# A two-layer encoder step on Trainium2: where the turned k and v tiles are emptied relative to the exponentials, and which bank the first v turn uses

## The chip, the cores and the metric

The kernel runs on one core of one Trainium2 chip. The metric is the device time of one execution in microseconds (us). Before the change it was 2435.56 us, the median of 3 runs (2432.95 to 2436.89).

A core has TensorE (PE in the profile; its weight loads are PEld), VectorE (DVE), ScalarE (ACT), GpSimd (POOL), and SyncE (SP), which only issues DMAs here. Each takes its own instructions in the order in which they are written. The engines keep each other in order by semaphores only.

## The reference

Two token groups (512 prompt tokens and 32 sample tokens with a cache of 256) pass through two layers. Each layer is SwiGLU, a mixer, SwiGLU, each with norms and gains. The first layer's mixer is "ab": eight heads of band attention with a relative-position bias (a) and four heads of differential attention (b). The second layer's is "c": sixteen heads of causal attention with a forget bias. The keys and values are results too, with tokens in rows.

```
proj = h @ w_in                      # q, k, v of every head
s = q @ k.T * 64 ** -0.5 + bias      # a: relative position, b: ALiBi, c: forget
p = softmax(s)                       # b: p0 - lam * p1
out = (p @ v) @ w_out
new = (k, v)                         # also returned
```

## The kernel before

Everything is held with features on the partitions and 544 tokens in the free dimension. A weight tile is split into a high and a low part (`split` and `half_split`: ACT writes `w_hi`, DVE the rest `w_lo`), and every product is three matmuls, written for two halves of 272 tokens.

Each mixer runs in nine **stages** (`Stage`, `st` 0 to 8). Stage `st` projects k, v and q of the head pair `st` (`lin_chunk`, three units of eight tiles), and at the same time attends with the head pair `st - 1`. In mixer ab the attending kind alternates: stages 1, 3, 5, 7 are a, stages 2, 4, 6, 8 are b. In mixer c all of 1 to 8 are c. Stage 0 only projects (`head`), stage 8 only attends. So 14 stages both project and attend: 4 of kind a, 3 of kind b, 7 of kind c.

A stage is a loop over steps `s` = 0 to 15 on each engine, and the order within a step is written out by hand. Steps 0 to 3 project k, 4 to 7 v, 8 to 11 q, two tiles a step. On PE a step is: the two tiles, `transpose_probs` of attention tile `s - lag` (lag 2, in b 3, where only odd tiles are turned), the products with v (`values` or `pair_values`), and in even steps below 10 `scores(s)` and `scores(s + 1)`. On ACT `exps(s)`, which is the exponential of tile `s`, and after it `split_next` (in steps 4, 5, 8, 9 half a weight tile) end the step.

Besides that each stage has three **turns** (`turn` on PE, `empty_turn` on ACT). k (`kT`), then v (`vT`), is transposed by four matmuls with the identity, and ACT copies it into `k_nat` or `v_nat`; the third turn does the sample's 32 rows and the cache's keys (`ckT`). Before, PE does them at the head of steps 5, 9 and 12, and ACT empties them at the head of the same steps, so behind the exponential and the weight half of the step before. All turns and all transposed probabilities go through one PSUM bank, `ps_t`. `tr_plan` numbers them, `wait_tr` makes PE wait until ACT has emptied the one before (semaphore `tr_out`), and `tr_ps` tells ACT that one is written. `ps_o`, another bank, takes the products with v.

The lines of the profile of before: L1278 the projection's matmuls, L1300 the turns of k and v, L1303 and L1306 the third turn, L1328 the scores, L1349 the transposes of probabilities, L1377 and L1400 the products with v, L1478 a turn of the forget terms, L1528 the weight half on ACT, L1829 the copies into `k_nat` and `v_nat`, L1841 the copy of transposed probabilities, L1853 the exponential, L1960 a whole `w_lo`, L2434 the row maximum for which the exponential waits.

Of the kernel before, what the change touches and what calls it, by code (L numbers as in the profile page):

```python
# [17 lines left out]
P = 128  # L18
# [7 lines left out]
QT = SEQ // P  # L26
# [191 lines left out]
def program(nc, ins, outs):  # L218
# [43 lines left out]
    with ExitStack() as ctx:  # L262
# [395 lines left out]
        def by_vector(n):  # L658
# [331 lines left out]
        def _(pe):  # L990
# [270 lines left out]
            def stage(st):  # L1261
# [22 lines left out]

                def turn(step):

                    new, base = st.new, st.at("tr")
                    if st.st == 0 and step == 5:
                        pe.wait_ge(pre_done, 2 * KT * (st.j + 1))
                    if step == 5:  # L1290
                        pe.wait_ge(kv_evac, evs + 1)
                        src = kT[:, new, :]
                    elif step == 9:
                        pe.wait_ge(kv_evac, evs + 2)
                        src = vT[:, :]
                    n = tr_plan(st).index((step, "turn"))
                    wait_tr(base + n)
                    if step in (5, 9):
                        for t in range(QT):
                            m = nc.tensor.transpose(ps_t[:, t * P:(t + 1) * P], src[:, t * P:(t + 1) * P], ident[:])  # L1300
                    else:
                        pe.wait_ge(cache_k[new], 16 * (st.same_new + 1))
                        nc.tensor.transpose(ps_t[0:DEC, 0:P], kT[:, new, SEQ:TOK], ident[:])  # L1303
                        nc.tensor.transpose(ps_t[0:DEC, P:2 * P], vT[:, SEQ:TOK], ident[:])
                        for c in range(2):
                            m = nc.tensor.transpose(ps_t[:, (2 + c) * P:(3 + c) * P], ck_nat[:, new, c, :], ident[:])  # L1306
                    m.then_inc(tr_ps, 1)
# [114 lines left out]
                if st.st == 0:  # L1422
                    head(st.j, st.kind)
                    if st.kind == "c":
                        pe.wait_ge(var_done, 2 * st.j + 2)
                        pe.wait_ge(fl_in, 32)
                        for t in range(2):
                            m = nc.tensor.transpose(ps_s[0:16, 0, t * P:(t + 1) * P], clf_nat[:, t, :], ident[:])
                        m.then_inc(fl_ps, 1)
                    for s in (5, 9, 12):  # L1430
                        turn(s)
                    return

                for s in range(STEPS + 2):
                    if st.new is not None and s in (5, 9, 12):
                        turn(s)
                    for part_half in (0, 1):
                        if st.new is not None and s < LIN_STEPS:
                            lin_chunk(s, part_half)
                        if st.st == 8 and part_half == 0:  # L1440
                            for m, k in OUT_PART[st.kind].get(s, ()):
                                if k == 0:
                                    pe.wait_ge(kv_evac, evs)
                                if k == OUT_LAST[st.kind]:
                                    pe.wait_ge(o_lo_done, st.at("ot"))
                                if k > OUT_LAST[st.kind]:
                                    pe.wait_ge(o_lo_done, st.at("ot") + 2 * (k - OUT_LAST[st.kind]))
                                out_part(st.j, m, k)
                    j = s - lag
# [60 lines left out]
        def _(act):  # L1510
# [279 lines left out]
            def first_stage(st, evac, empty_turn):  # L1790
# [9 lines left out]
                split(("q", j, 1, 0))  # L1800
                for s in (5, 9, 12):
                    empty_turn(s)

# [6 lines left out]
            def stage(st):  # L1810
# [10 lines left out]

                def empty_turn(step):
                    n = plan_t.index((step, "turn"))
                    act.wait_ge(tr_ps, st.at("tr") + n + 1)
                    if step in (5, 9):
                        if step == 5:
                            act.wait_ge(kv_stored[st.new], 64 * st.same_new)
                        dst = (k_nat if step == 5 else v_nat)[:, st.new, 0:QT, :].rearrange("p t n -> p (t n)")
                        nc.scalar.activation(dst, ps_t[:, :], ACT.Copy).then_inc(tr_out, 1)  # L1829
                    else:  # L1830
# [4 lines left out]
                def empty_probs(j, q, lag):  # L1835
                    t = order[j][0]
                    act.wait_ge(tr_ps, st.at("tr") + plan_t.index((j + lag, "probs")) + 1)
                    if q >= 2:
                        act.wait_ge(pv_done, st.at("pv") + (q - 1 if att == "b" else q // 2))
                    if t < QT:  # L1840
                        nc.scalar.activation(probsT[:, q % 2, 0:t + 1, :].rearrange("p b n -> p (b n)"),  # L1841
                                             ps_t[:, 0:(t + 1) * P], ACT.Copy).then_inc(tr_out, 1)
                    else:
                        nc.scalar.activation(probsT[:, q % 2, 0:2, 0:DEC],
                                             ps_t[:, 0:2 * P].rearrange("p (b n) -> p b n", b=2)[:, :, 0:DEC], ACT.Copy)
                        nc.scalar.activation(probsT[0:DEC, q % 2, 2, 0:DEC], ps_t[0:DEC, 2 * P:2 * P + DEC], ACT.Copy)\
                            .then_inc(tr_out, 1)
# [37 lines left out]
                for s in range(STEPS + 2):  # L1885
# [4 lines left out]
                    if st.new is not None:  # L1890
                        if s in (4, 8, 12):
                            evac(s // 4 - 1)
                        if s in (5, 9, 12):
                            empty_turn(s)
                    if st.st == 8 and s in (3, 6):
# [721 lines left out]
```

## Time and profile before

| | us |
|---|---|
| median of the runs | 2435.56 |
| the profiled execution's own time | 2436.59 |
| its span, first to last instruction | 2434.8 |
| PE busy | 2332.7 (96%) |
| DVE busy | 1443.0 (59%) |
| ACT busy | 911.1 (37%) |
| PE idle before L1349, ended by the copies of k and v | 15.4 |

The span is 1.8 us below the execution's own time; that rest lies around the instructions and the change has no part in it. The mixers lie at about 490 to 755 us (ab) and 1680 to 1960 us (c) of the span. A wait in brackets in a timeline row is idle time of that engine just before the row's first instruction, with the instruction that ended it. One row can stand for several instructions (the number behind the x). Matmul rows overlap their neighbours, since their ends are modelled.

### The profile page before, as it was taken

The numbers are of one execution on the slowest core, as the hardware profiler recorded it, in microseconds if no ns is written. First come the engines' busy times: TensorE is split into PE (matmuls) and PEld (weight loads), VectorE is DVE, ScalarE is ACT, GpSimd is POOL, SyncE is SP. The second block draws the span as 40 slices with busy tenths as digits, with TensorE's granted clock in tenths as the row PEclk, the third lists the DMA queues.
The fourth block names the chain that finished last, engine by engine and source line by source line (L and its number), as shares of the span: only waits on it lengthen the run. The fifth ranks groups of instructions, "written<-read, shape, count | busy, mean of one in ns | idle before, by whom it ended". The sixth has DMA issues, their size and how long they took to land.

```text
span 2434.8 us, 45695 instructions
## 1 busy us (share of the span) xinstructions
PE 2332.7 (96%) x18984; PEld 2220.9 (91%) x18984; DVE 1443.0 (59%) x2607; ACT 911.1 (37%) x1968; POOL 307.0 (13%) x369
## 2 busy tenths in 40 slices
PE   7999999999998999999999999997999899999998
PEld 4999999978877999999999999996777789999998
DVE  4577758655567756667566565756555575543223
ACT  4322232455556422222442222334555564222232
POOL 0000002411103300001220000232111151000001
PEclk9999999999999999999999999998999999999999
DMA  7455545322223144445514454442233221432321
GB/s 246 125 165 170 168 133 166 106 71 71 75 62 99 42 122 147 144 123 166 156 36 147 136 151 130 147 125 70 78 94 98 81 88 53 139 105 87 97 86 55
DMA packets 392701, 277.68 MB, mean 114 GB/s; under 512 B 11104, under 2 KB 349824, under 8 KB 392496
## 3 DMA queue, kind: packets, MB, share of 16 engines
q1 hardware_dynamic: 385792, 254.77, 35.4%
q0 software_dynamic: 6704, 19.99, 2.8%
q8 instruction: 151, 2.47, 0.4%
q14 instruction: 54, 0.44, 0.1%
HBM read 263.48 MB, written 12.81 MB: 113 GB/s over the span
## 4 chain that ended last, share of the span: by engine, by line
PE 83%; DVE 8%; ACT 3%; issue 3%; DMA 2%; POOL 1%; SPq 0%; ACTq 0%; DVEq 0%; POOLq 0%
PE lin L1021 62%; PE lin L1278 9%; PE lin L1041 2%; PE ps_s L1328 2%; PE ps_o L1400 2%; PE ps_t L1349 1%; DVE neg_max L2434 1%; DVE acc L1999 1%; DMA raw<-in_ffn_w_down 1%; DVE x L2084 1%; DVE probs L2426 1%; PE ps_s L1097 1%; DVE sums L2046 1%; DVE h_lo L2111 1%; PE ps_o L1377 1%
## 5 line engine op out<-in xcount | busy, mean ns | idle before, releaser
L1021 PE MATMUL lin<-h_hi,w_hi 128*128 128x272 f32 x2640 | 566.7, 290 | 4.0 <-ACT work L1600 2.1
L1021 PE MATMUL lin<-h_hi,w_lo 128*128 128x272 f32 x2640 | 564.3, 289 | 0.0
L1021 PE MATMUL lin<-h_lo,w_hi 128*128 128x272 f32 x2640 | 562.0, 288 | 0.0
L1960 DVE TENSOR_TENSOR w_lo<-raw,w_hi 128x1024 fp32r<-128x1024 f32 (+1 forms) x263 | 319.4, 1219 | 308.8 <-ACT w_hi L1520 307.4
L1021 PEld LDWEIGHTS lin<-h_hi,w_hi 128*128 128x128 f32 x2640 | 421.4, 189 | 6.5 <-ACT work L1600 2.8
L1021 PEld LDWEIGHTS lin<-h_lo,w_hi 128*128 128x128 f32 x2640 | 421.9, 189 | 0.0
L1021 PEld LDWEIGHTS lin<-h_hi,w_lo 128*128 128x128 f32 x2640 | 419.1, 189 | 0.0
L1520 ACT ACTIVATE w_hi<-raw 128x1024 fp32r<-128x1024 f32 (+1 forms) x263 | 269.9, 1036 | 181.0 <-DMA raw<-in_ffn_w_down 142.1
L1999 DVE SCALAR_TENSOR_TENSOR acc<-raw,silu_c,acc 128x512 f32<-128x512 f32 x448 | 313.8, 760 | 0.0
L1021 PE MATMUL lin<-act_hi,w_hi 128*128 128x272 f32 x1296 | 285.4, 290 | 5.5 <-DVE w_lo L1960 5.5
L1021 PE MATMUL lin<-act_hi,w_lo 128*128 128x272 f32 x1296 | 282.5, 289 | 0.0
L1021 PE MATMUL lin<-act_lo,w_hi 128*128 128x272 f32 x1296 | 282.1, 288 | 0.0
L1609 ACT ACTIVATE act_hi<-work 128x544 fp32r<-128x544 f32 (+1 forms) x100 | 60.4, 604 | 462.6 <-DVE work L2141 462.6
L1021 PEld LDWEIGHTS lin<-act_hi,w_hi 128*128 128x128 f32 x1296 | 208.9, 190 | 6.5 <-DVE w_lo L1960 5.7
L1021 PEld LDWEIGHTS lin<-act_lo,w_hi 128*128 128x128 f32 x1296 | 209.6, 189 | 0.0
L1021 PEld LDWEIGHTS lin<-act_hi,w_lo 128*128 128x128 f32 x1296 | 208.8, 190 | 0.0
L1278 PE MATMUL lin<-h_hi,w_hi 128*128 128x272 f32 x672 | 155.4, 313 | 1.8 <-DVE w_lo L1972 0.9
L1853 ACT ACTIVATE probs<-probs,neg_max 128x512 f32<-128x512 f32 (+4 forms) x160 | 89.1, 557 | 180.3 <-DVE neg_max L2434 179.6
L1600 ACT ACTIVATE work<-lin 128x544 f32<-128x544 f32 (+1 forms) x100 | 56.7, 567 | 263.7 <-PE lin L1021 263.7
L2141 DVE TENSOR_TENSOR work<-work,lin 128x544 f32<-128x544 f32 (+1 forms) x100 | 65.2, 652 | 134.0 <-PE lin L1021 133.3
L1278 PE MATMUL lin<-h_hi,w_lo 128*128 128x272 f32 x672 | 140.7, 291 | 0.0
L1278 PE MATMUL lin<-h_lo,w_hi 128*128 128x272 f32 x672 | 140.3, 291 | 0.0
(323 smaller groups left out, 3467.2 us busy)
## 6 DMA issues: line engine op xcount, KB each, us to landing
raw<-in_w_ada SPq DMA_DIRECT2D x128, 512.0 KB, 3.8
raw<-in_ffn_w_gate SPq DMA_DIRECT2D x88, 512.0 KB, 3.9
raw<-in_ffn_w_up SPq DMA_DIRECT2D x88, 512.0 KB, 3.9
raw<-in_ffn_w_down SPq DMA_DIRECT2D x64, 448.0 KB, 4.2
raw<-in_ffn_w_down SPq DMA_DIRECT2D x32, 512.0 KB, 4.9
raw<-in_w_in_ab SPq DMA_DIRECT2D x24, 512.0 KB, 3.8
raw<-in_w_in_c SPq DMA_DIRECT2D x24, 512.0 KB, 3.8
start_w<-in_w_ada SPq DMA_DIRECT2D x16, 512.0 KB, 11.9
```

The costliest lines, as they stand in the source:

```text
L1021: m = nc.tensor.matmul(out[a], w_tile(w, k), mv[:, k0 + k, half(a)], start=first and k == 0 and n == 0, stop=last and k == u["tiles"] - 1 ...
L1041: m = nc.tensor.matmul(out, w_tile(w, k), mv[:, k, half(a)], start=k == 0 and n == 0, stop=k == KT - 1 and n == 2)
L1278: m = nc.tensor.matmul(lin[:, 2 * out + a, 0:HALF], w[:, kt, :], mv[:, kt, half(a)], start=kt == 0 and n == 0, stop=kt == KT - 1 and n == 2)
L1328: m = nc.tensor.matmul(ps_s[0:r, j % 2, 0:keys(t)], lhs, kT[hs, par, 0:keys(t)], start=True, stop=True)
L1400: m = nc.tensor.matmul(ps_o[hs, c], lhs, rhs, start=b == 0, stop=b == blocks - 1)
L1520: nc.scalar.activation(w_all(dst, u["tiles"]), raw_all(u, dst), ACT.Copy).then_inc(hi_done, 1)
L1600: nc.scalar.activation(hidden_work(i), gate_out(i, False), ACT.Silu).then_inc(gate_read, 1)
L1609: nc.scalar.activation(act_hi[:, f, columns(halves)], work[:, f % 2, columns(halves)], ACT.Copy)\
L1853: nc.scalar.activation(probs[0:r, j % PSLOTS, 0:n], probs[0:r, j % PSLOTS, 0:n], ACT.Exp, bias=neg_max[0:r, j:j + 1], accum_out=row_sum[0: ...
L1960: nc.vector.tensor_tensor(w_all(w_l, u["tiles"]), raw_all(u, w_l), w_all(w_h, u["tiles"]).bitcast(F32), ALU.subtract).then_inc(lo_done, 1)
L1999: i = nc.vector.scalar_tensor_tensor(acc[:, g, :], w[:, r // 2, :], silu_c[:, kt, g:g + 1], acc[:, g, :], ALU.mult, ALU.add)
L2141: nc.vector.tensor_tensor(hidden_work(i), hidden_work(i), gate_out(i, True), ALU.mult).then_inc(prod_done, 1)
```

## The change

On ACT, the copies of k and v move from the head of steps 5 and 9 to the tail of steps 4 and 8, in front of that step's exponential and weight half. The third copy stays in step 12, behind the copy of q. On PE the turns are written at the tail of steps 4, 8 and 11, behind the scores, where they were written at the head of steps 5, 9 and 12; with nothing between a tail and the next head, PE's sequence is the same in every stage from 1 on. In stage 0 the turn of v goes into `ps_o` in place of `ps_t`, and waits no longer for the copy of k; the third turn then waits for the copy of k only.

```diff
+TURN_STEPS = (4, 8, 11)
@@ tr_plan
             for s in range(STEPS + 2):
-                if st.new is not None and s in (5, 9, 12):
-                    found.append((s, "turn"))
                 j = s - lag
                 if st.att is not None and 0 <= j < 10 and (st.att != "b" or j % 2):
                     found.append((s, "probs"))
+                if st.new is not None and s in TURN_STEPS:
+                    found.append((TURN_STEPS.index(s), "turn"))
+        def turn_bank(st, i):
+            return ps_o if st.st == 0 and i == 1 else ps_t
@@ PE, turn
-                    n = tr_plan(st).index((step, "turn"))
-                    wait_tr(base + n)
-                    if step in (5, 9):
+                    n = tr_plan(st).index((i, "turn"))
+                    if turn_bank(st, i) is ps_t:
+                        wait_tr(base + (1 if st.st == 0 and i == 2 else n))
+                    if i < 2:
                         for t in range(QT):
-                            m = nc.tensor.transpose(ps_t[:, t * P:(t + 1) * P], src[:, t * P:(t + 1) * P], ident[:])
+                            m = nc.tensor.transpose(turn_bank(st, i)[:, t * P:(t + 1) * P], src[:, t * P:(t + 1) * P],
+                                                    ident[:])
@@ PE, the steps
-                    if st.new is not None and s in (5, 9, 12):
-                        turn(s)
...
                     if s < 10 and s % 2 == 0:
                         scores(s)
                         scores(s + 1)
+                    if st.new is not None and s in TURN_STEPS:
+                        turn(TURN_STEPS.index(s))
@@ ACT, the steps
                         if s in (4, 8, 12):
                             evac(s // 4 - 1)
-                        if s in (5, 9, 12):
-                            empty_turn(s)
+                        if s == 12:
+                            empty_turn(2)
...
+                    if st.new is not None and s in TURN_STEPS[0:2]:
+                        empty_turn(TURN_STEPS.index(s))
                     if s < 10:
                         exps(s)
                     split_next(half_split, st, s)
```

The rest of the diff is in names and in how loops are written, with no effect on any engine's sequence.

ACT in a stage of kind c (mixer c, stage 3), steps 4 and 5, before. `probsT` are emptied transposes, `probs,row_sum` the exponential, `o_hi` a result of the attention:

```order
L1860 ACTIVATE inv_t<-ps_o 128x128
L1841 ACTIVATE probsT<-ps_t 128x384
L1853 ACTIVATE probs,row_sum<-probs,neg_max 128x256
L1528 ACTIVATE w_hi<-raw 128x512
L1829 ACTIVATE k_nat<-ps_t 128x512
L1867 ACTIVATE o_hi<-o_nat 128x128
L1841 ACTIVATE probsT<-ps_t 128x384
```

The same place of the changed kernel, whose line numbers are a few higher:

```order
L1868 ACTIVATE inv_t<-ps_o 128x128
L1849 ACTIVATE probsT<-ps_t 128x384
L1836 ACTIVATE k_nat<-ps_t 128x512
L1861 ACTIVATE probs,row_sum<-probs,neg_max 128x256
L1535 ACTIVATE w_hi<-raw 128x512
L1875 ACTIVATE o_hi<-o_nat 128x128
L1849 ACTIVATE probsT<-ps_t 128x384
```

The copy into `k_nat` has moved two rows up, past one exponential and one weight half. In step 8 the copy into `v_nat` moves the same way, and so in all 14 stages that project and attend.

PE at the end of stage 0 of mixer ab, before:

```order
L1300 MATMUL ps_t<-ident,kT 128x128 x4
L1300 MATMUL ps_t<-ident,vT 128x128 x4
L1303 MATMUL ps_t<-ident,kT 32x128
L1304 MATMUL ps_t<-ident,vT 32x128
L1306 MATMUL ps_t<-ident,ck_nat 128x128 x2
```

And in the changed kernel:

```order
L1306 MATMUL ps_t<-ident,kT 128x128 x4
L1306 MATMUL ps_o<-ident,vT 128x128 x4
L1310 MATMUL ps_t<-ident,kT 32x128
L1311 MATMUL ps_t<-ident,vT 32x128
L1313 MATMUL ps_t<-ident,ck_nat 128x128 x2
```

Nothing has moved on PE; the turn of v has another bank, here and in stage 0 of mixer c.

## Rows read from the trace of the kernel before

**Rows 1.** The page: busy time by engine, and the chain's shares by engine.

```profile
PE 2332.7 (96%) x18984; PEld 2220.9 (91%) x18984; DVE 1443.0 (59%) x2607; ACT 911.1 (37%) x1968; POOL 307.0 (13%) x369
...
PE 83%; DVE 8%; ACT 3%; issue 3%; DMA 2%; POOL 1%; SPq 0%; ACTq 0%; DVEq 0%; POOLq 0%
```

**Rows 2.** Line L1349: PE's idle time before it, by releaser: us, times.

```profile
  ACT v_nat L1829: 8.9, 11
...
  ACT k_nat L1829: 6.5, 11
```

**Rows 3.** Timeline, kind c, steps 4 to 6: start, length, engine, line, [idle before <-releaser].

```profile
1775.92 0.63 PE L1300 MATMUL ps_t<-ident,kT 128*128 128x128 f32 x4 [0.22 <-ACT probsT L1841]
...
1777.04 0.51 ACT L1853 ACTIVATE probs<-probs,neg_max 128x256 f32<-128x256 f32 x1 [1.26 <-DVE neg_max L2434]
...
1777.55 0.62 ACT L1528 ACTIVATE w_hi<-raw 128x512 fp32r<-128x512 f32 x1
...
1778.07 0.57 ACT L1829 ACTIVATE k_nat<-ps_t 128x512 f32<-128x512 f32 x1
...
1778.79 0.52 PE L1349 MATMUL ps_t<-ident,probs 128*128 128x128 f32 x3 [0.73 <-ACT k_nat L1829]
...
1779.34 0.49 ACT L1841 ACTIVATE probsT<-ps_t 128x384 f32<-128x384 f32 x1 [0.50 <-PE ps_t L1349]
...
1780.64 0.38 PE L1349 MATMUL ps_t<-ident,probs 128*128 128x128 f32 x2
```

**Rows 4.** Timeline, kind c, the same stage, steps 8 and 9.

```profile
1787.68 0.63 PE L1300 MATMUL ps_t<-ident,vT 128*128 128x128 f32 x4
...
1788.91 0.54 ACT L1853 ACTIVATE probs<-probs,neg_max 32x288 f32<-32x288 f32 x1 [1.38 <-DVE neg_max L2434]
...
1789.97 0.57 ACT L1829 ACTIVATE v_nat<-ps_t 128x512 f32<-128x512 f32 x1
...
1790.68 0.30 PE L1349 MATMUL ps_t<-ident,probs 128*128 128x128 f32 x1 [0.88 <-ACT v_nat L1829]
```

**Rows 5.** Timeline, kind a (mixer ab, stage 3), steps 4, 5 and 9.

```profile
579.38 0.63 PE L1300 MATMUL ps_t<-ident,kT 128*128 128x128 f32 x4 [0.22 <-ACT probsT L1841]
...
580.11 0.51 ACT L1853 ACTIVATE probs<-probs,neg_max 128x256 f32<-128x256 f32 x1 [0.87 <-DVE neg_max L2434]
...
581.86 0.52 PE L1349 MATMUL ps_t<-ident,probs 128*128 128x128 f32 x3 [0.34 <-ACT k_nat L1829]
...
593.37 0.30 PE L1349 MATMUL ps_t<-ident,probs 128*128 128x128 f32 x1 [0.73 <-ACT v_nat L1829]
```

**Rows 6.** Timeline, kind b (mixer ab, stage 2), steps 4 to 6.

```profile
545.34 0.51 ACT L1853 ACTIVATE probs<-probs,neg_max 128x256 f32<-128x256 f32 x1
...
545.60 0.63 PE L1300 MATMUL ps_t<-ident,kT 128*128 128x128 f32 x4 [1.54 <-ACT probsT L1841]
...
549.83 0.51 ACT L1853 ACTIVATE probs<-probs,neg_max 128x256 f32<-128x256 f32 x1 [2.88 <-DVE neg_max L2434]
...
549.97 0.49 PE L1349 MATMUL ps_t<-ident,probs 128*128 128x128 f32 x3
```

**Rows 7.** Timeline, mixer ab, end of stage 0 and first matmuls of stage 1.

```profile
496.53 1.23 DVE L1960 TENSOR_TENSOR w_lo<-raw,w_hi 128x1024 fp32r<-128x1024 f32 x1 [3.52 <-ACT w_hi L1520]
...
497.06 0.63 PE L1300 MATMUL ps_t<-ident,vT 128*128 128x128 f32 x4 [1.57 <-ACT k_nat L1829]
...
498.75 0.50 PE L1278 MATMUL lin<-h_hi,w_hi 128*128 128x272 f32 x2
```

**Rows 8.** Timeline, mixer c, behind stage 0: PE's next work after the turns.

```profile
1684.87 0.63 PE L1478 MATMUL ps_s<-ident,logf 16*128 16x16 f32 x5 [2.75 <-DVE decay L2567]
```

**Rows 9.** Windows of 5 us where stages 2, 4, 6 end (kind b); PEclk third from last.

```profile
563.00:568.00 5.00, 4.62 (x23) 3.44 (x22) 0.28 (x1) 0.98 (x6) 3.94 (x6) 0.68 0.69 198
630.00:635.00 5.00, 4.62 (x30) 3.19 (x31) 0.87 (x3) 0.98 (x6) 3.76 (x6) 1.00 0.72 209
696.00:701.00 5.00, 4.73 (x22) 3.15 (x22) 0.28 (x1) 3.78 (x9) 4.05 (x6) 0.69 0.69 194
```

More of the change, by code:

```diff
@@ L1283, in lin_chunk, with turn @@
                         assert ws.count[u["name"], 0] == steps[0], u["name"]
-                def turn(step):
+                def turn(i):
                     new, base = st.new, st.at("tr")
-                    if st.st == 0 and step == 5:
+                    if st.st == 0 and i == 0:
                         pe.wait_ge(pre_done, 2 * KT * (st.j + 1))
-                    if step == 5:
+                    if i == 0:
                         pe.wait_ge(kv_evac, evs + 1)
                         src = kT[:, new, :]
-                    elif step == 9:
+                    elif i == 1:
                         pe.wait_ge(kv_evac, evs + 2)
                         src = vT[:, :]
-                    n = tr_plan(st).index((step, "turn"))
-                    wait_tr(base + n)
-                    if step in (5, 9):
+                    n = tr_plan(st).index((i, "turn"))
+                    if turn_bank(st, i) is ps_t:
+                        wait_tr(base + (1 if st.st == 0 and i == 2 else n))
+                    if i < 2:
                         for t in range(QT):
-                            m = nc.tensor.transpose(ps_t[:, t * P:(t + 1) * P], src[:, t * P:(t + 1) * P], ident[:])
+                            m = nc.tensor.transpose(turn_bank(st, i)[:, t * P:(t + 1) * P], src[:, t * P:(t + 1) * P],
+                                                    ident[:])
                     else:
@@ L1429, in stage @@
                         m.then_inc(fl_ps, 1)
-                    for s in (5, 9, 12):
-                        turn(s)
+                    for i in range(3):
+                        turn(i)
                     return
                 for s in range(STEPS + 2):
-                    if st.new is not None and s in (5, 9, 12):
[L1436 to L1448, printed above, removed]
+                    if st.new is not None and s < LIN_STEPS:
+                        lin_chunk(s, 0)
+                        lin_chunk(s, 1)
+                    if st.st == 8:
+                        for m, k in OUT_PART[st.kind].get(s, ()):
+                            if k == 0:
+                                pe.wait_ge(kv_evac, evs)
+                            if k == OUT_LAST[st.kind]:
+                                pe.wait_ge(o_lo_done, st.at("ot"))
+                            if k > OUT_LAST[st.kind]:
+                                pe.wait_ge(o_lo_done, st.at("ot") + 2 * (k - OUT_LAST[st.kind]))
+                            out_part(st.j, m, k)
                     j = s - lag
@@ L1800, in first_stage @@
                 split(("q", j, 1, 0))
-                for s in (5, 9, 12):
-                    empty_turn(s)
+                for i in range(3):
+                    empty_turn(i)
             def forget_act():
@@ L1820, in evac, with empty_turn @@
                                          scale=HD ** -0.5 if k == 2 else 1.0).then_inc(kv_evac, 1)
-                def empty_turn(step):
-                    n = plan_t.index((step, "turn"))
+                def empty_turn(i):
+                    n = plan_t.index((i, "turn"))
                     act.wait_ge(tr_ps, st.at("tr") + n + 1)
-                    if step in (5, 9):
-                        if step == 5:
+                    if i < 2:
+                        if i == 0:
                             act.wait_ge(kv_stored[st.new], 64 * st.same_new)
-                        dst = (k_nat if step == 5 else v_nat)[:, st.new, 0:QT, :].rearrange("p t n -> p (t n)")
-                        nc.scalar.activation(dst, ps_t[:, :], ACT.Copy).then_inc(tr_out, 1)
+                        dst = (v_nat if i else k_nat)[:, st.new, 0:QT, :].rearrange("p t n -> p (t n)")
+                        nc.scalar.activation(dst, turn_bank(st, i)[:, :], ACT.Copy).then_inc(tr_out, 1)
                     else:
@@ L1839, in empty_probs @@
                         act.wait_ge(pv_done, st.at("pv") + (q - 1 if att == "b" else q // 2))
+                    dst = probsT[:, q % 2]
                     if t < QT:
-                        nc.scalar.activation(probsT[:, q % 2, 0:t + 1, :].rearrange("p b n -> p (b n)"),
+                        nc.scalar.activation(dst[:, 0:t + 1, :].rearrange("p b n -> p (b n)"),
                                              ps_t[:, 0:(t + 1) * P], ACT.Copy).then_inc(tr_out, 1)
                     else:
-                        nc.scalar.activation(probsT[:, q % 2, 0:2, 0:DEC],
+                        nc.scalar.activation(dst[:, 0:2, 0:DEC],
                                              ps_t[:, 0:2 * P].rearrange("p (b n) -> p b n", b=2)[:, :, 0:DEC], ACT.Copy)
-                        nc.scalar.activation(probsT[0:DEC, q % 2, 2, 0:DEC], ps_t[0:DEC, 2 * P:2 * P + DEC], ACT.Copy)\
+                        nc.scalar.activation(dst[0:DEC, 2, 0:DEC], ps_t[0:DEC, 2 * P:2 * P + DEC], ACT.Copy)\
                             .then_inc(tr_out, 1)
```

1 line of the change is left out of this document (removed).

## The prediction

> **What bounds the kernel now.** I read the page first: PE is busy 96% of the span, and the chain that ended last is 83% PE [rows 1]. Nothing but PE can be the bound for long, so an edit is worth what it takes out of PE's idle time or adds to it. Next I read the line whose work shares a bank with the turns: L1349, the transposes of the probabilities. PE stood idle before it for 8.9 us in 11 places until ACT had copied v, and for 6.5 us in 11 places until ACT had copied k [rows 2]. 11 is the number of stages that project and attend with kind a or c (4 + 7); the three of kind b are not among them. Then I read one stage of each kind as a timeline. The stages repeat closely: 7 waits of 0.73 and 4 of 0.34 give 6.5 for k, 7 of 0.88 and 4 of 0.73 give 9.1 for v, against 6.5 and 8.9 in rows 2, so one stage of each kind stands for all [rows 2 to 5].
>
> What the reader is to see in the kind c stage [rows 3]: PE ends the turn of k at 1775.92 + 0.63 = 1776.55. ACT is idle then: the exponential's row says that it waited 1.26 us, until 1777.04, for a row maximum. It runs the exponential, then a weight half (to 1778.17), and only then the copy of k, to 1778.64. PE has been ready for the next transpose since 1778.79 - 0.73 = 1778.06. So the copy sits for a microsecond and a half behind work that is not urgent, while its bank is what PE wants next.
>
> **The change, part by part.**
>
> *PE.* In the 14 stages from 1 on PE's sequence is the same, and the turns wait for the same things. Cost and gain nothing by themselves. The third turn and its copy do not move on any engine; nor do POOL's and SP's queues and their DMAs.
>
> *The copy of k in kind c, 7 times.* ACT can start it when the turn is written. ACT follows a PE end by about 0.03 us (1778.79 + 0.52 = 1779.31, and the copy behind it starts at 1779.34 [rows 3]), so it runs from 1776.58 to 1777.15. The exponential cannot start before 1777.04, when its maximum is there; it now starts near 1777.06 to 1777.15, so it is at most 0.1 us late. The copy lies in ACT's idle time. PE is ready at 1778.06, 0.9 us after the copy has ended, and so the 0.73 us go. What is late next? PE's transpose of step 6, at 1780.64, would come at 1779.91. It needs the copy of the one before, which ended at 1779.34 + 0.49 = 1779.83 and will itself move up with PE and by the 0.57 us that have left ACT's queue there. Even unmoved it is 0.08 us early. Its exponential, at 1777.7, is two microseconds early. I count the full 0.73.
>
> *The copy of v in kind c, 7 times.* The turn ends at 1787.68 + 0.63 = 1788.31, the copy takes 1788.34 to 1788.91, and the exponential started at 1788.91 anyway, when its maximum was there [rows 4]. Nothing is delayed. PE is ready at 1790.68 - 0.88 = 1789.80, 0.9 us after the copy's end. The full 0.88 goes.
>
> *Kind a, 4 times.* The turn of k ends at 580.01, the copy runs 580.04 to 580.61, and the exponential (before at 580.11) starts 0.5 us late. Its user, the transpose of step 6, comes two microseconds after PE's ready time 581.86 - 0.34 = 581.52, so this delay has cover. The copy's end leaves 0.9 us of slack, and 0.34 goes. At v the wait of 0.73 goes in the same way as in kind c [rows 5].
>
> *Kind b, 3 times.* Here the added wait shows. PE starts the turn of k only at 545.60, itself released by an ACT copy, and ends it at 546.23. ACT ran the exponential at 545.34, before that turn had even begun [rows 6]. Now ACT must stand idle until 546.26, copy, and start the exponential near 546.8, 1.4 us later; behind it in the queue the weight half is as late. Who waits? ACT's next work is the exponential at 549.83, which had waited 2.88 us for its maximum [rows 6]; with 1.4 us taken from it, 1.5 us are left. PE's transpose at 549.97 had no idle time before it and takes an older tile, and the copy of k is done three microseconds ahead. So this is neither gain nor loss: 0, with up to 1.4 each as the bound if the cover were not there. At v in kind b I find the exponential 0.1 us late and nobody waiting.
>
> *Stage 0 of mixer ab.* The turn of v waited 1.57 us for the copy of k [rows 7]. Now it follows the turn of k at once, and the third turn starts when the copy of k is done, at 497.06, where the turn of v stood. What is late next is not the bank: stage 1's first matmul at 498.75 needs `w_lo`, done at 496.53 + 1.23 = 497.76. It moves to about 497.8. I count 0.9 us. Bounds: 0, if something later in stage 1 takes it back, and 1.3, if the weights did not matter.
>
> *Stage 0 of mixer c.* The same edit, but PE then waits 2.75 us for DVE's forget chain until 1684.87 [rows 8]. The gain only lengthens that wait: 0.
>
> *The sum*: 8.9 + 6.5 + 0.9 = 16.3 us. The profiled execution took 2436.59, its span and 1.8 us around it; less 16.3 that is 2420.3. It lies 1.0 us above the median of the runs, 2435.56, so against the median I expect 2435.56 - 16.3 = 2419.3.
>
> **A rule of the skill that speaks against this.** In rows 6 the copy, once it is written first, holds the exponential up although that is ready. The Trainium skill, PSUM — Partial Sum Buffer, section "Engine vs sequencer instructions", says "ScalarE/VectorE/GpSimdE queues are strict FIFO", so every copy put ahead of an exponential makes it wait for PE's turn. If each such delay reached PE, the sum would lose 3 x 1.4 + 4 x 0.5 + 7 x 0.1 = 6.9 us; the rows show other work over each of them, so I leave it out of the sum.
>
> **The clock.** The granted clock is 0.68 of full speed in the window where stage 2 ends and 0.69 where stage 6 ends, but 1.00 where stage 4 ends, though the three run the same instructions [rows 9]. PE has just had the waits at the end of a stage of kind b in all three. A low window costs 5 x 0.32 = 1.6 us. Which of the three fall low can change when everything moves by 2 to 4 us: from all three low (+1.6) to none (-3.1). The Trainium skill, TensorE: Matmul & The Clock Gate, section "Part 1: The HAM clock gate", says that the clock follows how busy the array has been recently; by it a kernel with fewer stalls can only win here, and that is the second case below.
>
> **The rivals, and how the numbers follow.** A measurement of this kernel can tell about 0.2% (4.9 us) from no change.
>
> - *All 22 waits go* (0.65): 2419.3.
> - *They go, and the low windows at the ends of stages 2 and 6 too* (0.14): 3.1 us less, 2416.2. For it: stage 4 shows that full clock is possible there. Against it: the waits just ahead of those windows are not touched.
> - *Half of it comes back* (0.11). The waits for k go, but those for v turn up again in the next transposes, which wait for ACT's copy of the one before, or the other way round. For it: the margin of 0.08 us above if ACT's queue did not move up. Against it: it does move up. 2435.56 - 6.5 - 0.9 = 2428.2, or with the v waits alone 2425.8.
> - *The change does nothing that counts* (0.06): PE's sequence is the same, and a later wait of each stage (for `w_lo`, or for the last row maximum) takes everything back. Then 2435, from 2431 to 2437.
> - *Slower* (0.04): the exponential behind the copy becomes the bound in kind b and a. Place: step 4. Price: 3 x 1.4 + 4 x 0.5 = 6.2 us with no gain elsewhere, 2441.8. It decides from the point at which ACT's wait of 2.88 us in rows 6 is shorter than 1.4 us; the trace has twice that.
>
> The predicted time is that of the first case, 2419.3. The range: below, the clock's best case and one more microsecond of scatter (the runs of before lie 2.6 us under to 1.3 us over their median), 2415; above, a third low window, scatter and the case in which only the v waits go, 2426. That holds the first two cases nearly whole and half of the third. Faster by over 0.2%: 0.65 + 0.14 + 0.11 = 0.90. Within 0.2%: 0.06. Slower: 0.04.
>
> **What would show it.** Right: in the idle time before the transposes of probabilities the two entries for the copies of k and v are gone, and no other releaser there has grown by more than a microsecond or two; in a stage of kind c the copy of k starts about 0.03 us after the turn and ends before its exponential starts; two successive stages of kind c lie about 1.6 us closer together than before; in kind b ACT waits near 0.8 us for the turn and the wait before the exponential of step 5 has shrunk to about 1.5 us; stage 1 of mixer ab begins 0.9 us earlier after the turn of k; the third turn of stage 0 in mixer c is earlier and the wait of 2.75 us longer. Wrong: a wait of PE for the copy of transposed probabilities or for an exponential in steps 6 or 10 that before was not there, or a granted clock below 1.00 in windows of the mixers where it was full.

## The result and the profile after

The changed kernel took 2414.72 us, the median of 4 runs (2412.73 to 2415.77), against 2435.47 us of the kernel before on the same chip (4 runs). The ratio is 0.9915, with a 95% interval from 0.9903 to 0.9927: faster by 20.75 us, where 16.3 us had been predicted. 2414.72 lies 0.28 us under the low end of the predicted range.

The page of after, engines and chain, answers to [rows 1]:

```profile
PE 2323.7 (96%) x18984; PEld 2217.1 (92%) x18984; DVE 1443.7 (60%) x2607; ACT 909.0 (38%) x1968; POOL 307.5 (13%) x369
...
PE 85%; DVE 7%; ACT 2%; issue 2%; DMA 2%; POOL 1%; SPq 0%; ACTq 0%; DVEq 0%; POOLq 0%
```

PE is still the bound. The 22 waits of [rows 2] are gone. Line L1349 is now L1356; PE's idle time before it, by releaser (us, times):

```profile
  ACT probs L1861: 9.0, 5
  DVE probs L2461: 2.8, 5
  ACT probsT L1849: 2.7, 3
```

No entry for `k_nat` or `v_nat` is left, and none has taken their place. The waits of PE in the whole span show it line by line (us in total, times, longest). First three of before, then three of after:

```profile
PE ps_t L1300 <- ACT probsT L1841: 7.2, 15, 1.5
...
PE ps_t L1300 <- ACT k_nat L1829: 2.9, 2, 1.6
...
PE ps_t L1349 <- ACT probsT L1841: 2.7, 3, 1.7
```

```profile
PE ps_t L1306 <- ACT probsT L1849: 7.2, 15, 1.5
...
PE ps_t L1356 <- ACT probsT L1849: 2.7, 3, 1.7
...
PE ps_t L1310 <- ACT k_nat L1836: 1.9, 2, 1.0
```

The waits for transposed probabilities stand at the same sums and counts. The two waits of the v turn in the stages 0 (2.9 us) have given way to two of the third turn (1.9 us). Before, the third turn also waited there for the copy of v, 1.4 us in two places, so 4.3 us before stand against 1.9 after.

The stage of kind c that [rows 3] shows, after, steps 4 to 6:

```profile
1761.78 0.63 PE L1306 MATMUL ps_t<-ident,kT 128*128 128x128 f32 x4 [0.22 <-ACT probsT L1849]
...
1762.44 0.60 ACT L1836 ACTIVATE k_nat<-ps_t 128x512 f32<-128x512 f32 x1 [0.81 <-PE ps_t L1306]
...
1762.93 0.50 ACT L1861 ACTIVATE probs<-probs,neg_max 128x256 f32<-128x256 f32 x1
...
1763.49 0.42 PE L1283 MATMUL lin<-h_hi,w_lo 128*128 128x272 f32 x2
...
1763.75 0.49 PE L1356 MATMUL ps_t<-ident,probs 128*128 128x128 f32 x3
...
1764.00 0.49 PE L1283 MATMUL lin<-h_hi,w_hi 128*128 128x272 f32 x2
```

The turn ends at 1762.41 and the copy starts 0.03 us later. The exponential follows it 1.15 us after the turn's start (1.12 before: 1777.04 - 1775.92), so it is hardly late. In kind a it follows by 1.15 us too, against 0.73 before [rows 5]: it is 0.4 us late, and no transpose waits for it. PE runs from the last projection matmul into the transpose without a bracket.

**How far apart stages lie** is the measure that the rest leans on. ACT's copy of q stands once in every stage that projects and attends. Before and after, in two successive stages of kind c:

```profile
1760.78 0.60 ACT L1819 ACTIVATE qT<-lin 128x544 f32<-128x544 f32 x1
...
1795.54 0.60 ACT L1819 ACTIVATE qT<-lin 128x544 f32<-128x544 f32 x1
```

```profile
1746.65 0.60 ACT L1826 ACTIVATE qT<-lin 128x544 f32<-128x544 f32 x1
...
1779.43 0.60 ACT L1826 ACTIVATE qT<-lin 128x544 f32<-128x544 f32 x1
```

A stage of kind c took 34.76 us and takes 32.78, which is 1.98 less. All six such distances before are 34.74 to 34.77; after, five are 32.77 to 32.79 and the last is 32.95. (In the last one PE waits 0.19 us before the turn of v, before and after. Before, the wait for the copy of v was shorter by as much there, 0.69 in place of 0.88, so this stage gained 0.16 less. The ranges for c below leave this last distance out where it is longer.) Taken the same way in mixer ab, at full clock, a stage of kind a took 35.34 (stage 5) and takes 33.92, 1.42 less, and kind b stays at 30.3 (30.26 to 30.31 before, 30.28 to 30.30 after). The prediction had 1.61 for c (0.73 + 0.88) and 1.07 for a (0.34 + 0.73). So 7 x 1.97 + 4 x 1.42 + 0.94 for stage 0 (below) = 20.4 us, less the 0.16 of the last stage 20.2 us, with the medians at 20.75.

The profiled executions differ by more: 2436.59 against 2412.73 us of own time, 23.9 us. The rest of 3.6 us isn't the change's. 1.5 of it is the clock in mixer ab: two low windows before [rows 9], one after. 1.3 lies ahead of the mixers and 1.3 between mixer ab and stage 1 of mixer c, in stretches where the change has no instruction; against that, 0.5 less than in the sum was saved from stage 0's first copy of q in mixer ab to stage 1's. The last copy of q and the span's end are 500.2 us apart in both.

### The profile page after: what moved, and what is told of

Its sections match the earlier page's. It is cut to its first block, busy times and chain, and to the rows that moved or that the text cites. A ratio compares the mean times of both kernels' runs of the same rounds, so it can differ in the third digit from the quotient of the medians.

```text
span 2410.9 us, 45693 instructions
## 1 busy us (share of the span) xinstructions
PE 2323.7 (96%) x18984; PEld 2217.1 (92%) x18984; DVE 1443.7 (60%) x2607; ACT 909.0 (38%) x1968; POOL 307.5 (13%) x369
## 4 chain that ended last, share of the span: by engine, by line
PE 85%; DVE 7%; ACT 2%; issue 2%; DMA 2%; POOL 1%; SPq 0%; ACTq 0%; DVEq 0%; POOLq 0%
PE lin L1026 62%; PE lin L1283 10%; PE lin L1046 2%; PE ps_o L1407 2%; PE ps_s L1335 2%; PE ps_t L1356 1%; DVE acc L2009 1%; PE ps_t L1306 1%; DVE x L2094 1%; DMA raw<-in_ffn_w_down 1%; DVE neg_max L2444 1%; PE ps_s L1102 1%; DVE sums L2056 1%; DVE h_lo L2121 1%; ACT w_hi L1527 1%
```

## The experiments

The question is where 20.2 us come from when the brackets removed add up to 15.4 and stage 0 was taken as 0.9. **Theory 1:** each of the 22 waits cost PE more than its bracket, by a fixed bit of about 0.17 us. **Theory 2:** the waits cost their brackets, and the rest came from elsewhere, from stage 0 or the clock. The diffs are against the changed kernel unless said otherwise. "Distance" is that between successive copies of q.

### Without the bank edit of stage 0

```diff
-            return ps_o if st.st == 0 and i == 1 else ps_t
+            return ps_t
@@
-                        wait_tr(base + (1 if st.st == 0 and i == 2 else n))
+                        wait_tr(base + n)
```

> The changed kernel without its stage 0 part: the turn of v in stage 0 uses the shared bank and waits as before; only the copies of k and v on ACT are moved. Theory 1 (a wait costs PE what its bracket shows plus about 0.17 us, because the bracket counts from the modelled end of the matmul before, while the next matmul could have started 0.17 us ahead of that end): 15.4 + 22 x 0.17 = 19.2 us below before, 2416.3. Theory 2 (the brackets are the whole cost, and what the change gained beyond 16.3 us came from the clock windows in mixer ab): 15.4 below before plus or minus one or two clock windows of 1.6 us, 2417 to 2422, and a period of kind c stages 1.61 us below the 34.75 us of before. By theory 1 that period falls by 1.97 us. Both: 0.9 us slower than the changed kernel from stage 0.

Measured: 2414.71 us (2412.38 to 2416.49) against 2436.55, ratio 0.9909 (0.9894 to 0.9924). The time is that of the changed kernel, 1.6 us under what theory 1 gave; within the scatter of the runs it can't show the 0.9 us. The trace can: in mixer ab from the start of the turn of k in stage 0 to stage 1's first projection matmul it is 3.86 us, as before, against 2.92 after. The distances are the changed kernel's, 32.75 to 32.78 for c and 33.90 for a. So the excess isn't stage 0's; it sits inside the stages.

### The bank edit of stage 0 alone

```diff
+                        if s == 5:
+                            empty_turn(0)
+                        if s == 9:
+                            empty_turn(1)
@@
-                    if st.new is not None and s in TURN_STEPS[0:2]:
-                        empty_turn(TURN_STEPS.index(s))
```

> The kernel before with the stage 0 part alone: the turn of v in its own bank, the copies of k and v on ACT where they were. Both theories: 0.9 us below before, 2434.6, which one run cannot tell from no change; in the trace, the first projection matmul of stage 1 in mixer ab comes 0.9 us sooner after the turn of k, now released by the split weights, and PE's wait for the forget chain behind stage 0 of mixer c grows from 2.75 to about 4.1 us. Rival: the gain is more than 1.5 us, then the stage 0 part holds what was missing in the prediction.

Measured: 2432.84 us (2431.52 to 2436.75), ratio 0.9984 (0.9975 to 0.9994) against 2436.55. The medians say 3.7 us, with an interval from 1.5 to 6.1; the trace says 0.94: 2.92 us in place of 3.86 at the end of stage 0 of mixer ab, and distances like those of before (34.73 to 34.75 for c). By the medians alone this is the rival's case, a gain above 1.5 us. Against it stands the kernel above, which has no bank edit and yet the changed kernel's time. In the changed kernel the same place reads so, start, length and idle time before:

```profile
494.14 0.60 PE L1306 MATMUL ps_t<-ident,kT 128*128 128x128 f32 x4
...
494.58 0.60 PE L1306 MATMUL ps_o<-ident,vT 128*128 128x128 f32 x4
...
496.22 0.28 PE L1310 MATMUL ps_t<-ident,kT 128*32 128x128 f32 x1 [1.05 <-ACT k_nat L1836]
...
497.06 0.52 PE L1283 MATMUL lin<-h_hi,w_hi 128*128 128x272 f32 x2 [0.23 <-DVE w_lo L1970]
```

The weights end the last wait, as predicted. In stage 0 of mixer c the gain is absorbed, here and after; the row of after that answers to [rows 8]:

```profile
1674.59 0.63 PE L1485 MATMUL ps_s<-ident,logf 16*128 16x16 f32 x5 [4.17 <-DVE decay L2577]
```

The wait was 2.75. That stage 0 of c gives nothing is the same in both kernels with the edit. The part of the 3.7 us above 0.94 has no place in the trace; but that is the trace of the slowest of the ten executions (2436.75 us), and it can't speak for the median. The mean granted clock that was recorded with every execution says more: in the median it was 0.989 over the 13 of the kernel before and 0.991 over these ten. In another group of the kernel before, the two with the lowest and the highest clock, 0.987 and 0.994, took 2437.5 and 2429.33 us, which makes 1.2 us for 0.001. By that estimate some 2 of the 2.8 us are the clock's. Why it differed isn't shown.

### The copies behind the exponential, ahead of the weight half

```diff
-                    if st.new is not None and s in TURN_STEPS[0:2]:
-                        empty_turn(TURN_STEPS.index(s))
                     if s < 10:
                         exps(s)
+                    if st.new is not None and s in TURN_STEPS[0:2]:
+                        empty_turn(TURN_STEPS.index(s))
                     split_next(half_split, st, s)
```

> The changed kernel with the copies of k and v between the exponential and the weight half: behind the exponential, ahead of the half. From the rows of before, in kind c the copy of k would end at 1778.12 and PE start at 1778.27, the copy of v at 1790.02 and PE at 1790.17; in kind a only v is late, by a copy ending at 592.72. Theory 1 (PE could have gone on at 1777.89, 1789.63 and 592.47): 7 x (0.38 + 0.54) + 4 x 0.40 = 8.0 us above the changed kernel, 2422.7. Theory 2 (1778.06, 1789.80, 592.64): 7 x (0.21 + 0.37) + 4 x 0.23 = 5.0 us above, 2419.7. If neither the order of copy and exponential nor the weight half matters, it equals the changed kernel, 2414.7.

Measured: 2422.54 us (2421.19 to 2424.2), ratio 0.9942 (0.9927 to 0.9957). Distances for c are 33.70 to 33.71, which is 0.93 above the changed kernel; theory 1 had said 0.92 and theory 2 0.58. For a they are 34.32 to 34.33, 0.40 above, where the theories had said 0.40 and 0.23. The kind c stage again:

```profile
1768.25 0.51 ACT L1861 ACTIVATE probs<-probs,neg_max 128x256 f32<-128x256 f32 x1 [1.25 <-DVE neg_max L2444]
...
1768.75 0.58 ACT L1836 ACTIVATE k_nat<-ps_t 128x512 f32<-128x512 f32 x1
...
1768.85 0.41 PE L1283 MATMUL lin<-h_hi,w_lo 128*128 128x272 f32 x2
...
1769.47 0.52 PE L1356 MATMUL ps_t<-ident,probs 128*128 128x128 f32 x3 [0.21 <-ACT k_nat L1836]
```

From the last projection row to the transpose it is 0.62 us here and 0.26 after (1763.49 to 1763.75). So 0.36 us were lost behind a bracket of 0.21. That is theory 1 in four rows. It also shows that the exponential, not only the weight half, has to be passed: half of the gain hangs on it.

### Kind c alone

The copies move in mixer c only, and stage 0 keeps the bank of before (as in the first experiment; not repeated in the cut below).

```diff
+                        if s == 5 and st.kind != "c":
+                            empty_turn(0)
+                        if s == 9 and st.kind != "c":
+                            empty_turn(1)
@@
-                    if st.new is not None and s in TURN_STEPS[0:2]:
+                    if st.kind == "c" and st.new is not None and s in TURN_STEPS[0:2]:
                         empty_turn(TURN_STEPS.index(s))
```

> The kernel before with the copies of k and v moved in mixer c alone: mixer ab, where the low clock windows lie, and stage 0 are as before. Theory 1 (bracket plus 0.17 us a wait): 7 x (0.90 + 1.05) = 13.7 us below before, 2421.8. Theory 2 (the brackets alone): 7 x (0.73 + 0.88) = 11.3 us below, 2424.2. In the trace the period of the kind c stages is 32.8 us by theory 1 and 33.15 us by theory 2.

Measured: 2421.99 us (2421.36 to 2423.54) against 2435.2, ratio 0.9948 (0.9935 to 0.996). That is 13.2 us, where theory 1 counts 7 x 1.97 = 13.8 and theory 2 7 x 1.61 = 11.3. The time leans to the first but its interval (9.7 to 15.8 us) holds both. The distances decide: 32.76 to 32.81 for c, where brackets alone would make 33.15. Theory 1.

### The copy of k in kind c alone

```diff
                         if s == 5 and st.kind != "c":
                             empty_turn(0)
-                        if s == 9 and st.kind != "c":
+                        if s == 9:
                             empty_turn(1)
@@
-                    if st.kind == "c" and st.new is not None and s in TURN_STEPS[0:2]:
-                        empty_turn(TURN_STEPS.index(s))
+                    if st.kind == "c" and st.new is not None and s == 4:
+                        empty_turn(0)
```

(against the kernel just above)

> The kernel before with the copy of k alone moved, in mixer c alone; v as before. Theory 1: 7 x 0.90 = 6.3 us below before, 2429.2, and the wait for the copy of v still shows 0.88 in its bracket. Theory 2: 7 x 0.73 = 5.1 us, 2430.4. If part of the gain in kind c comes from k and v together (an earlier exponential or a result copied earlier), the period falls by less than 0.90 us.

Measured: 2430.09 us (2425.2 to 2432.31), ratio 0.9979 (0.997 to 0.9989). The time can't decide between 2429.2 and 2430.4. The distances can: 33.83 to 33.85, 0.92 under before, with a bracket of 0.73. The v wait, left in place, therefore costs the other 1.06 with a bracket of 0.88. Each wait has the same excess, 0.18 to 0.19.

### Kind b back as it was

```diff
+                        if s == 5 and att == "b":
+                            empty_turn(0)
+                        if s == 9 and att == "b":
+                            empty_turn(1)
@@
-                    if st.new is not None and s in TURN_STEPS[0:2]:
+                    if att != "b" and st.new is not None and s in TURN_STEPS[0:2]:
                         empty_turn(TURN_STEPS.index(s))
```

> The changed kernel with the copies in the three projecting kind b stages put back behind exponential and weight half. As predicted, kind b neither gains nor loses: equal to the changed kernel within a clock window of 1.6 us, 2413 to 2416.5, and PE's timeline of a kind b stage is the same to 0.1 us. Rival: ACT standing idle for the turn costs 1.4 us a stage, then this kernel is 4.2 us faster than the changed one; or kind b hid a gain, then it is slower by more than 1.6 us.

Measured: 2414.48 us (2410.0 to 2417.66), ratio 0.992 (0.9905 to 0.9935), and 30.29 us for kind b as in both kernels. The edit is neutral there. In the changed kernel, kind b (mixer ab, stage 2), steps 3 to 5:

```profile
541.76 0.59 ACT L1849 ACTIVATE probsT<-ps_t 128x512 f32<-128x512 f32 x1
...
543.16 0.60 ACT L1836 ACTIVATE k_nat<-ps_t 128x512 f32<-128x512 f32 x1 [0.81 <-PE ps_t L1306]
...
543.65 0.50 ACT L1861 ACTIVATE probs<-probs,neg_max 128x256 f32<-128x256 f32 x1
...
546.73 0.51 ACT L1861 ACTIVATE probs<-probs,neg_max 128x256 f32<-128x256 f32 x1 [1.97 <-DVE neg_max L2444]
```

ACT stands idle for 0.81 us with a ready exponential behind the copy. The next exponential's wait has shrunk from 2.88 us [rows 6] to 1.97, so the delay ends in idle time and reaches nobody.

### Kind b: the first probabilities emptied a step earlier

PE waits 1.54 us in each kind b stage before the turn of k [rows 6], because ACT's exponential of step 3 stands ahead of the copy of transposed probabilities. This kernel empties both `kT` and those probabilities ahead of that exponential.

```diff
-                        if s in (4, 8, 12):
+                        if s in (4, 8, 12) and not (early and s == 4):
                             evac(s // 4 - 1)
@@
-                    if 0 <= j < 10 and (att != "b" or j % 2):
+                    if 0 <= j < 10 and (att != "b" or j % 2) and not (early and s == 4):
                         empty_probs(j, j // 2 if att == "b" else j, lag)
@@ at the end of the step, ahead of exps(s); early is st.new is not None and att == "b"
+                    if early and s == 3:
+                        evac(0)
+                        empty_probs(1, 0, lag)
```

> The changed kernel, and in the three kind b stages that also project, ACT copies k out of its accumulator and empties the first transposed probabilities ahead of the exponential of step 3 in place of behind it. Theory 1: PE's wait of 1.54 us before the turn of k shrinks to about 0.2 us; with the hidden 0.17 that is 3 x 1.5 = 4.5 us below the changed kernel, 2410.2. Theory 2: 3 x 1.3 = 4.0 us, 2410.7; the two are not told apart by it. Rival: the exponential of step 3, 0.2 us later, or the next row maximum becomes the bound and nothing is gained, 2414.7.

Measured: 2409.41 us (2406.75 to 2412.2), ratio 0.9888 (0.9873 to 0.9903). Kind b stages take 28.89 us, 1.39 less, between the 1.5 and the 1.3 of the two theories. One row of its waits of PE shows what went; it stood at 7.2, 15, 1.5 in both kernels:

```profile
PE ps_t L1306 <- ACT probsT L1849: 2.6, 12, 0.2
```

Three waits of 1.54 are gone, and twelve of 0.22 stay, eleven of them before the turn of k in kinds a and c. Here the gain is below the bracket. Kind b, steps 3 and 4:

```profile
540.10 0.70 PE L1335 MATMUL ps_s<-kT,qT 64*128 64x256 f32 x4
540.21 0.60 ACT L1849 ACTIVATE probsT<-ps_t 128x512 f32<-128x512 f32 x1 [1.65 <-PE ps_t L1356]
...
540.95 0.63 PE L1306 MATMUL ps_t<-ident,kT 128*128 128x128 f32 x4
```

The copy ends at 540.81, and the turn follows the start of the scores by 0.85 us, though without a bracket. The next kernel has 0.64 for the same pair where nothing waits, so 0.21 of the old wait is left. A gain of 1.39 with 0.21 left makes 1.60 for a wait with a bracket of 1.54. So the excess of 0.17 isn't a constant to add to any bracket: what stands ahead of this wait are score matmuls, and there it is about 0.06.

### The probabilities' copy ahead of the reciprocals' copy

On top of the last kernel, for kinds a and c, where the eleven waits of 0.22 are left:

```diff
-                    j = s - lag - 1
-                    if att != "b" and 0 <= j < 10 and j % 2:
-                        inv_copy(j // 2)
                     j = s - lag
                     if 0 <= j < 10 and (att != "b" or j % 2) and not (early and s == 4):
                         empty_probs(j, j // 2 if att == "b" else j, lag)
+                    j = s - lag - 1
+                    if att != "b" and 0 <= j < 10 and j % 2:
+                        inv_copy(j // 2)
```

> The kernel with the early copies of kind b, and on top of it, in kinds a and c, ACT empties the transposed probabilities ahead of the copy of the reciprocals in each step in place of behind it. PE's wait before the turn of k in these kinds shows 0.22 us in its bracket, 11 times. Theory 1 (bracket plus 0.17 us): 11 x 0.39 = 4.3 us below the kernel with the early copies alone, and the period of the kind c stages falls from 32.78 to 32.4 us. Theory 2 (the bracket alone): 11 x 0.22 = 2.4 us, period 32.56 us. Rival: the copy of the reciprocals, now later, holds up DVE and the next exponential, and the period does not fall.

Measured: 2407.78 us (2404.77 to 2410.89) against 2431.74 (9 runs), ratio 0.9898 (0.9883 to 0.9912). Distances for c are 32.44 to 32.48, 0.32 under the changed kernel: between the two expectations, 0.39 and 0.22. First the row of its waits, then the scores and the turn:

```profile
PE ps_t L1306 <- ACT probsT L1849: 0.2, 1, 0.2
```

```profile
1757.67 0.70 PE L1335 MATMUL ps_s<-kT,qT 64*128 64x256 f32 x4
1758.31 0.66 PE L1306 MATMUL ps_t<-ident,kT 128*128 128x128 f32 x4
```

The turn starts 0.64 us after the scores; before it was 0.91 (1775.01 to 1775.92). That is 0.27 for a bracket of 0.22, an excess of 0.05, and about another 0.05 lies in the rest of the stage. So behind score matmuls the excess is 0.05, and behind projection matmuls 0.17. The ratio is no better than the 0.9888 of the kernel above, and the two intervals overlap nearly whole: the times don't tell these two apart, and they were taken on different chips. The changed kernel was run beside this one (next section) and took 7.4 us more by the medians; the distances say 3 x 1.39 + 4 x 0.30 (33.62 for a) + 7 x 0.32 = 7.6. By the distances this is the shortest version of the study, and both lie below the changed kernel.

### The changed kernel once more

> The changed kernel itself, beside the one above on the same chip. Both theories: 20 to 21 us below the kernel before. In its trace the ends of the kind b stages 2, 4 and 6 of mixer ab show which of the three windows have a low clock; the stages of kind a behind a low one are 1.5 us longer than the others. If the low windows belong to the program, it is stage 4's again and no other; if they do not, it is another set.

Measured: 2415.18 us (2412.11 to 2416.22), ratio 0.9925 (0.9912 to 0.9939). Both theories had said 20 to 21 us under the kernel before; the medians say 16.6 (against 2431.74) and the recorded ratio 18.2, with an interval from 14.8 to 21.4, which holds 20.2. The distances say that the kernel is the same: those for c are 32.77 to 32.80 and those for a at full clock 33.93, as in the first execution (32.77 to 32.79, and 33.92). The windows at the ends of stages 2, 4 and 6, PEclk third from last; first the profiled execution of after, then this one:

```profile
558.00:563.00 5.00, 3.79 (x31) 2.90 (x29) 1.68 (x6) 2.30 (x10) 2.05 (x3) 1.00 0.51 150
624.00:629.00 5.00, 4.62 (x25) 3.31 (x24) 0.28 (x1) 0.98 (x6) 3.85 (x6) 0.71 0.70 202
690.00:695.00 5.00, 4.64 (x30) 3.34 (x31) 1.14 (x4) 3.86 (x9) 4.05 (x6) 1.00 0.65 183
```

```profile
558.00:563.00 5.00, 3.79 (x31) 3.04 (x30) 2.31 (x8) 3.15 (x15) 0.87 (x2) 1.00 0.36 105
624.00:629.00 5.00, 3.79 (x28) 2.57 (x26) 1.10 (x4) 1.93 (x10) 2.66 (x5) 1.00 0.57 161
690.00:695.00 5.00, 5.00 (x22) 3.31 (x22) 0.28 (x1) 3.50 (x7) 4.05 (x6) 0.66 0.67 189
```

The same program, and the low window has moved from stage 4 to stage 6.

## Why the prediction was right in kind and short in size

**Which waits go, and that nothing takes their place: right.** 22 waits gone, no other releaser before the transposes grown by more than a fraction of a microsecond, the copy 0.03 us behind the turn, the exponential not 0.1 us late. One reading was too quick: not every stage of kind c has a v wait of 0.88. The last has 0.69, which is why 7 x 0.88 + 4 x 0.73 gave 9.1 against the 8.9 of [rows 2]; the sum used 8.9. The rivals "half of it comes back", "nothing that counts" and "slower" are out.

**Kind b neutral: right**, with one size off. ACT's idle time before the copy is 0.81 us as predicted; the next exponential's wait is 1.97, not 1.5, because the exponential's delay of 1.4 us was taken as the whole queue's, though the copy itself, about 0.5 us of the queue (543.16 to 543.65), no longer stands behind it. The Trainium skill's rule that was weighed against the change (PSUM — Partial Sum Buffer, section "Engine vs sequencer instructions") agrees with the rows on the order, since ACT does stand with ready work in its queue; no delay reaches PE, and the 6.9 us that it would have taken are zero.

**Stage 0: right.** 0.94 us against 0.9 in mixer ab, ended by the weights as predicted; nothing in mixer c, where the wait grew from 2.75 to 4.17 us.

**What failed: the size of a wait.** The step is "PE has been ready for the next transpose since 1778.79 - 0.73 = 1778.06", and with it the first term of the sum, 8.9 + 6.5 = 15.4 us. It reads the bracket as the whole cost. The rows of before ahead of that wait, and the first projection row behind it:

```profile
1777.65 0.41 PE L1278 MATMUL lin<-h_hi,w_lo 128*128 128x272 f32 x2
1778.79 0.52 PE L1349 MATMUL ps_t<-ident,probs 128*128 128x128 f32 x3 [0.73 <-ACT k_nat L1829]
1779.06 0.49 PE L1278 MATMUL lin<-h_hi,w_hi 128*128 128x272 f32 x2
```

The first row holds two matmuls; the same row starts every 0.25 us along the projection, so one starts each 0.125 us and the second here at 1777.775. It ends at 1778.06 by its modelled length of 0.29, and from there the bracket counts. But PE could have started the next one at 1777.90. The wait therefore cost 0.73 + 0.16, and 0.02 more in the transposes themselves. Compared directly: from the last projection row ahead of the wait to the first behind it was 1779.06 - 1777.65 = 1.41 us and is 1764.00 - 1763.49 = 0.51, so 0.90 us for the k wait of kind c. With v's 1.06 that is the 1.97 of the distances. Over 22 waits the excess is 3.9 us; with it the sum would have been 20.2 us and the forecast 2415.4, 0.7 us above what was measured. The Trainium skill knows both lengths apart (TensorE: Matmul & The Clock Gate, sections "Single matmul latency" and "Back-to-back issue gap"): for 272 columns at full clock its formulas, written for bf16 matmuls and the second without the weight loads between them, give 279 and 116 ns as estimates, against 0.29 us and 0.125 us here.

The trace of before had this price in it, in the rows of the weight loads (PEld). First the loads for the two transposes of kind c; then PEld's idle time before all loads of this line, before and after. "issue" means that the profile shows nothing it waited for.

```profile
1778.76 0.31 PEld L1349 LDWEIGHTS ps_t<-ident,probs 128*128 128x128 f32 x3 [0.91 <-issue]
...
1790.65 0.14 PEld L1349 LDWEIGHTS ps_t<-ident,probs 128*128 128x128 f32 x1 [1.06 <-issue]
```

```profile
PEld ps_t L1349 <- issue: 21.9, 24, 1.9
```

```profile
PEld ps_t L1356 <- issue: 2.4, 2, 1.9
```

0.91 and 1.06 are what the k and the v wait of kind c cost by the distances, and 22 of these waits with 19.5 us are gone, against 15.4 + 3.9 = 19.3. Ahead of the turn of k, behind score matmuls, PEld has some idle time even where nothing waits, and the difference counts: 0.59 before and 0.33 with the probabilities' copy first in kind c (0.26, by the starts 0.27), 1.91 before and 0.52 with the early copies in kind b (1.39, as by the distances). The largest difference is in the kernel with the copies behind the exponential, 0.40 for the k wait of kind c where 0.36 was lost. Why the idle time of the loads comes so near the cost isn't shown.

**The range** failed for the same reason. Its low end was built from the clock and scatter alone, with the 15.4 us taken as exact. A second price for the same waits, from start to start, would have put it 4 us lower.

**The clock: half right.** One low window costs 1.5 to 1.6 us (kind a with one, 36.87 before and 35.49 after, against 35.34 and 33.92 without), as estimated. But the rival in which the change takes the low windows away has no ground: they move between executions of one program.

## What to carry to other kernels

A bracket is counted from the modelled end of the instruction before it, so it understates what a stall costs an engine whose instructions overlap; price a stall from the start of the last instruction ahead of it to the start of the first behind it, and take off what the same two lie apart where nothing waits. The idle time of the weight loads (PEld) is a second reading of it, and here it came within 0.04 us of the cost, once what it shows without a wait was taken off. When a kernel repeats its stages, the distance between two occurrences of one instruction tells 0.1 us apart where times of whole runs can't tell 1. As in this kernel, copies that free a bank for the bounding engine belong ahead of work that nobody waits for soon, also where the copying engine then idles, as long as its next work still has a wait of its own to absorb the delay.

## What the runs showed of the hardware that I had not expected

- The cost of a stall on PE goes beyond its idle bracket by 0.16 to 0.19 us behind 272-column matmuls, and by 0.05 to 0.06 us behind the 256-column score matmuls (64 rows).
- A low granted clock (0.66 to 0.71 in a window of 5 us) sat at the end of stage 2 and 6 (before), of 4 (after) and of 6 alone (the same program again). It was 2 alone with kind b back as it was, and by the distances none in three of the kernels tried. Each cost 1.5 to 1.6 us. I don't know what picks the stage.
- The distances of stages agree to 0.05 us between executions and chips, while the medians of the kernel before were 2436.55, 2435.20 and 2431.74 us in three groups, with median clocks of 0.989, 0.991 and 0.992, and the bank edit alone came out at 3.7 us by medians where its trace shows 0.94.
